# The delta rule without its matrix w: keys read the state, VectorE subtracts, one product with the inverse

## The reference, cut to what matters

```python
lower = where(strict, (k*beta) @ k.T * decay, 0)
rhs   = concat([v*beta, k*beta*exp(gc)])
u, w  = solve(lower + eye, rhs)          # the inverse applied to both halves
for c in chunks:                         # state is 128 x 128 per head
    v_new = u[c] - w[c] @ state
    o[c]  = q_dec[c] @ state + attn[c] @ v_new
    state = state * g_last[c] + k_dec[c].T @ v_new
```

## Time and profile before

| | |
|---|---|
| device time, median of 3 runs (lowest, highest) | 1108.64 us (1108.6, 1109.4) |
| span of the profiled execution | 1106.4 us |
| TensorE busy in it | 1086.0 us (98%) |
| VectorE, ScalarE, GpSimd busy | 603.2, 475.2, 480.6 us |
| head loop of the first mixer | from about 150 to 324 us; one head is 23.4 us |

### The profile page before, as it was taken

The page is one execution under the profiler, slowest core; times in us unless marked ns, Lnnn a source line. Parts: engine busy times, 40 slices in busy tenths (PEclk is TensorE's granted clock), DMA queues, the critical chain, the costliest instruction groups (busy, mean ns, idle before and its releaser), DMA issues. The chain is left out here.

```text
span 1106.4 us, 16476 instructions
## 1 busy us (share of the span) xinstructions
PE 1086.0 (98%) x5787; PEld 903.6 (82%) x5787; DVE 603.2 (55%) x1349; ACT 475.2 (43%) x1009; POOL 480.6 (43%) x276
## 2 busy tenths in 40 slices
PE   7999999999999999999999999999999999989996
PEld 6888899899988888888888888887788888767775
DVE  6677746666547555532122125536956666554667
ACT  6644345565534431431332234353434444454545
POOL 5785413222226684775575475356222122113130
PEclk9999999999999999999999999999999999999999
DMA  7544531211104444452541644604112011000011
GB/s 219 143 126 114 129 88 50 66 58 57 40 20 139 136 152 139 120 160 91 157 152 57 190 134 121 159 20 115 39 39 67 20 39 50 29 10 15 20 62 77
DMA packets 167158, 100.10 MB, mean 90 GB/s; under 512 B 30424, under 2 KB 160812, under 8 KB 166060
## 3 DMA queue, kind: packets, MB, share of 16 engines
q1 hardware_dynamic: 166924, 99.06, 31.1%
q10 hardware_dynamic: 160, 0.07, 0.0%
HBM read 95.69 MB, written 3.16 MB: 89 GB/s over the span
## 5 line engine op out<-in xcount | busy, mean ns | idle before, releaser
L1244 POOL TENSOR_TENSOR wlo<-stage,whi 128x1024 fp32r<-128x1024 f32 (+1 forms) x105 | 272.4, 2598 | 221.5 <-ACT whi L740 221.5
L2243 PE MATMUL ps<-hhi,whi 128*128 128x512 f32 (+1 forms) x728 | 311.5, 428 | 2.4 <-DVE gated L2005 1.9
L2243 PE MATMUL ps<-hhi,wlo 128*128 128x512 f32 (+1 forms) x728 | 294.0, 404 | 0.0
L2243 PE MATMUL ps<-hlo,whi 128*128 128x512 f32 (+1 forms) x728 | 285.1, 395 | 0.0
L2243 PEld LDWEIGHTS ps<-hhi,whi 128*128 128x128 f32 (+1 forms) x728 | 137.0, 188 | 37.3 <-issue 6.5
L2243 PEld LDWEIGHTS ps<-hhi,wlo 128*128 128x128 f32 (+1 forms) x728 | 137.3, 189 | 30.0 <-issue 6.3
L740 ACT ACTIVATE whi<-stage 128x1024 fp32r<-128x1024 f32 x104 | 109.7, 1056 | 121.0 <-PE ps L2243 89.0
L1342 POOL TENSOR_TENSOR wlo<-stage,whi 128x1024 fp32r<-128x1024 f32 (+3 forms) x40 | 73.4, 1835 | 194.3 <-ACT whi L1034 194.3
L2243 PEld LDWEIGHTS ps<-hlo,whi 128*128 128x128 f32 (+1 forms) x728 | 137.1, 188 | 24.0
L1122 ACT ACTIVATE prob<-ps,aneg 128x128 f32<-128x128 f32 (+1 forms) x96 | 50.9, 530 | 175.4 <-DVE aneg L2036 122.8
L2243 PE MATMUL ps<-ahi,whi 128*128 128x512 f32 x312 | 124.2, 398 | 0.0
(11 more groups left out here) (401 smaller groups left out, 1825.7 us busy)
## 6 DMA issues: line engine op xcount, KB each, us to landing
stage<-dn_w_in SPq DMA_DIRECT2D x32, 512.0 KB, 4.0
stage<-mlp_w_up SPq DMA_DIRECT2D x32, 512.0 KB, 4.3
stage<-mlp_w_down SPq DMA_DIRECT2D x32, 512.0 KB, 4.6
mod_w<-ada_w SPq DMA_DIRECT2D x8, 1536.0 KB, 6.5
stage<-w_in SPq DMA_DIRECT2D x17, 512.0 KB, 3.6
gcrow<-gc_rows SPq DMA_DIRECT2D x16, 256.0 KB, 3.5
stage<-dn_w_out SPq DMA_DIRECT2D x8, 512.0 KB, 3.6
stage<-w_in SPq DMA_DIRECT2D x9, 256.0 KB, 3.0
```

The lines of the kernel that those rows point to most:

```text
L1244: pool.tensor_tensor(wlo[:, slot, 0:ks, 0:cols], stage[:, slot, 0:ks, 0:cols], whi[:, slot, 0:ks, 0:cols], ALU.subtract).then_inc(s["w_lo" ...
L2243: mm = pe.matmul(bank, w[:, slot, k - ks[0], 0:width], x[:, k], start=(i == 0), stop=(i == len(todo) - 1))
```

## The change

w is not made any more: `w_product`, `w_out_`, `kbeta` and `wT` are gone. Instead, for each chunk c > 0, PE multiplies the keys by the state (`state_read`), DVE multiplies that by `kwgain` and subtracts `vbeta` (`less_read`, in place), and PE applies the inverse once (`v_new`); ACT's copy turns the sign. The head loop is written in another order on PE, ACT and DVE. The banks of finished projections are released after the taps and not after the silu.

```diff
+        def read_bank(h):
+            return 5 if h < H - 1 else 6
 ACT ----
-            def w_out_(g):
-                act.wait_ge(s["w_ps"], g + 1)
-                act.activation(wT[:, :, :], ps[:, 5, :].rearrange("p (c i) -> p c i", c=CH), ACT.Copy, scale=-1.0)\
-                    .then_inc(s["w_ev"], 1)
-
             def v_new(h, c):
                 act.wait_ge(s["v_ps"], h * 4 + c + 1)
-                act.activation(vnew[:, c, :], ps[:, 3, 0:P], ACT.Copy).then_inc(s["v_ev"], 1)
+                act.activation(vnew[:, c, :], ps[:, 3, 0:P], ACT.Copy, scale=-1.0 if c else 1.0).then_inc(s["v_ev"], 1)
 
             def o_first(h, c):
                 act.wait_ge(s["o1_ps"], h * 3 + c)
-                if h * 4 + c > 1:
+                if c > 1:
                     act.wait_ge(s["o_ready"], h * 4 + c)
+                elif h:
+                    act.wait_ge(s["o_ready"], h * 4)
...
                     tap0(f"q{g}")
+                o_first(h, 1)
+                v_new(h, 1)
+                if ahead:
+                    inv_32(g)
                     next_split(f"q{g}")
                 o_squares(h, 0)
-                v_new(h, 1)
-                if not ahead:
-                    out_hi(h - 1)
-                if ahead:
-                    inv_32(g)
-                o_first(h, 1)
+                o_first(h, 2)
+                v_new(h, 2)
                 if ahead:
                     conv_tanh(f"q{g}")
-                    q_squares(g)
+                    turned_64(g)
+                else:
+                    out_hi(h - 1)
                 o_squares(h, 1)
-                v_new(h, 2)
                 if ahead:
-                    turned_64(g)
-                o_first(h, 2)
-                if h and ahead:
-                    out_hi(h - 1)
-                o_squares(h, 2)
+                    tap0(f"v{g}")
+                o_first(h, 3)
                 v_new(h, 3)
                 if ahead:
-                    tap0(f"v{g}")
+                    q_squares(g)
                     next_split(f"v{g}")
                     conv_tanh(f"v{g}")
-                o_first(h, 3)
-                if ahead:
-                    w_out_(g)
+                    if h:
+                        out_hi(h - 1)
+                o_squares(h, 2)
                 o_squares(h, 3)
 DVE ----
-                dve.tensor_tensor(kbeta[:, :, :], kn, bc(kwgain[:, g], P), ALU.mult).then_inc(s["kside"], 1)
                 dve.tensor_tensor(kdec[:, :, :], kn, bc(gates[:, g, 2, :], P), ALU.mult).then_inc(s["kside"], 1)
...
+            def less_read(h, c):
+                dve.wait_ge(s["ks_ps"], h * 3 + c)
+                dve.wait_ge(s["vb_ready"], h + 1)
+                dve.scalar_tensor_tensor(out=vbeta[:, c], in0=ps[:, read_bank(h), 0:P], scalar=kwgain[:, h, c:c + 1], in1=vbeta[:, c],
+                                         op0=ALU.mult, op1=ALU.subtract).then_inc(s["rhs_ready"], 1)
...
+                less_read(h, 1)
                 out_rows(h, 0)
                 if ahead:
-                    taps(f"q{g}")
-                    inv_t_32(g)
-                else:
-                    out_gate(h - 1)
+                    taps(f"q{g}", (1, 2))
                 next_state(h, 1)
                 if ahead:
+                    taps(f"q{g}", (3,))
+                less_read(h, 2)
+                out_rows(h, 1)
+                if ahead:
+                    inv_t_32(g)
+                if h:
+                    out_gate(h - 1)
+                next_state(h, 2)
+                if ahead:
                     silu2(f"q{g}", qT[:, g % 2])
-                out_rows(h, 1)
-                next_state(h, 2)
-                if h and ahead:
-                    out_gate(h - 1)
+                less_read(h, 3)
                 out_rows(h, 2)
 PE ----
-            def w_product(g):
-                pe.wait_ge(s["l64_t"], g + 1)
-                pe.wait_ge(s["kside"], g * 2 + 1)
-                for c in range(CH):
-                    mm = pe.matmul(ps[:, 5, c * P:(c + 1) * P], kbeta[:, c], invT[:, g % 2, c], start=True, stop=True)
-                mm.then_inc(s["w_ps"], 1)
+            def state_read(h, c):
+                pe.wait_ge(s["st_ready"], h * 3 + c)
+                if h == H - 1:
+                    pe.wait_ge(s["attn_ready"], H)
+                pe.matmul(ps[:, read_bank(h), 0:P], chunk(kT[:, h], c), state[:, (c - 1) % 2], start=True, stop=True)\
+                    .then_inc(s["ks_ps"], 1)
...
-                elif c > 1:
-                    pe.wait_ge(s["o1_ev"], h * 3 + c - 1)
-                mm = pe.matmul(ps[:, 3, 0:P], invT[:, h % 2, c], vbeta[:, c], start=True, stop=(c == 0))
-                if c:
-                    pe.wait_ge(s["w_ev"], h + 1)
-                    pe.wait_ge(s["st_ready"], h * 3 + c)
-                    mm = pe.matmul(ps[:, 3, 0:P], wT[:, c], state[:, (c - 1) % 2], start=False, stop=True)
-                mm.then_inc(s["v_ps"], 1)
+                elif c:
+                    pe.wait_ge(s["o1_ev"], h * 3 + c)
+                    pe.wait_ge(s["rhs_ready"], h * 3 + c)
+                pe.matmul(ps[:, 3, 0:P], invT[:, h % 2, c], vbeta[:, c], start=True, stop=True).then_inc(s["v_ps"], 1)
...
                 o_rows(h, 0)
+                state_read(h, 1)
+                o_first(h, 1)
+                if ahead:
+                    level_32b(g)
+                fill(3)
                 v_new(h, 1)
-                if not ahead:
+                if h:
                     out_turn(h - 1)
-                if ahead:
-                    fill(2)
-                    level_32b(g)
-                fill(F_A if ahead else 3)
-                o_first(h, 1)
+                fill(F_A)
                 state_sum(h, 1)
                 fill(F_A)
                 o_rows(h, 1)
+                state_read(h, 2)
+                o_first(h, 2)
+                fill(3)
                 v_new(h, 2)
-                fill(2)
+                fill(3)
                 if ahead:
                     level_64a(g)
-                fill(F_A if ahead else 3)
-                o_first(h, 2)
                 state_sum(h, 2)
-                if h and ahead:
-                    fill(2)
-                    out_turn(h - 1)
                 fill(F_A)
                 o_rows(h, 2)
+                state_read(h, 3)
+                o_first(h, 3)
+                if ahead:
+                    level_64b(g)
+                fill(3)
                 v_new(h, 3)
                 if ahead:
-                    level_64b(g)
+                    k_rows(g)
                 fill(F_A)
-                if ahead:
-                    k_rows(g)
-                o_first(h, 3)
                 o_rows(h, 3)
                 fill(F_A)
                 if ahead:
                     qk_products(g)
-                    w_product(g)
                     q_sums(g)
```

More of the change, by code:

```diff
@@ L223, in build @@
         attnT = sb("attnT", [P, CH, P])
-        kbeta = sb("kbeta", [P, CH, P])
         kdec = sb("kdec", [P, CH, P])
         vbeta = sb("vbeta", [P, CH, P])
-        wT = sb("wT", [P, CH, P])
         vnew = sb("vnew", [P, CH, P])
@@ L351, in build @@
             lb_in lb_ps inv_step inv_out inv_in0 inv_in1 parts_ready inv_ready lev_ready base_ready
-            l32_ps l32_ev l32_r l32_inv l32_t l64_ps l64_ev l64_r l64_t kn_ps kside w_ps w_ev qk_ps attn_ready
+            l32_ps l32_ev l32_r l32_inv l32_t l64_ps l64_ev l64_r l64_t kn_ps kside ks_ps rhs_ready qk_ps attn_ready
             dmin q_sq qss_ps q_norm vn_ps vb_ready v_ps v_ev st_ps st_ready o_ps o1_ps o1_ev o_ready
@@ L916, in parts @@
                 if g >= 2:
-                    act.wait_ge(s["w_ps"], g - 1)
                     act.wait_ge(s["v_ps"], (g - 1) * 4)
@@ L933, in _ @@
             parts(1)
-            w_out_(0)
             for h in range(H):
@@ L1461, in _, with taps @@
             dve.tensor_scalar(V["dn_norm_w"], V["dn_norm_w"], 0.5 * float(P) ** -0.5, None, ALU.mult)
-            def taps(name):
+            def taps(name, which=(1, 2, 3)):
                 i, h, seq = CONV[name], int(name[1]), "qkv".index(name[0])
                 a, u = acc[:, i % 2], ps[:, bank_of_unit(name), :]
-                for t in range(1, 4):
+                for t in which:
                     dve.wait_ge(s["conv0"], i + 1) if t == 1 else dve.wait_ge(s["conv1"], i * 3 + t - 1)
@@ L2337, in consumed @@
                 else:
-                    pe.wait_ge(s["seq_ready"], CONV[name] + 1)
+                    pe.wait_ge(s["conv1"], CONV[name] * 3 + 3)
             def dn_unit(name):
@@ L2399, in fillers @@
                         if e < 2:
-                            pe.wait_ge(s["seq_ready"], CONV[("q7", "v7")[e]] + 1)
+                            pe.wait_ge(s["conv1"], CONV[("q7", "v7")[e]] * 3 + 3)
                         else:
-                            pe.wait_ge(*((s["w_ev"], H), (s["q_norm"], H))[e - 2])
```

(19 more changed lines are left out.)

## The result

The changed kernel takes 1115.9 us (median of 5 runs, 1114.9 to 1117.44) against 1108.64: a ratio of 1.0066, 95% interval 1.0055 to 1.0077. It is slower, by 7.3 us; the forecast was 1110.3 in a range up to 1113.1. The profiled execution has a span of 1115.6 us, 9.2 more than the one before.

The account below looks back on a forecast made before the run. TensorE was taken to bound the kernel, with no idle time in the head loop. -7.0 + 3.7 + 0.8 + 2.3 + 1.9 = +1.7 us on the 1106.4 span, median 2.2 above: 1110.3 us, range 1105.5 to 1113.1.

Parts of the forecast that it names:

- The clock falls (slower): Rival: TensorE's clock falls at the head 6 or end wait, +1.7 (1112.0), both 1113.7; swinging clock 1124; chance 0.14.
- the waits that I had counted: TensorE waits on o1, on vbeta, before k-tile 5 and before k-tile 7: +3.7, +0.8, +2.3 and +1.9 us.
- are as long as that pair, but with full work right up to them: New waits, 2.3 us (head 6) and 2.0 (end), compared with second-block idles of 1.89 and 0.82 us, where the clock fell.
- w products gone: TensorE: eight w products of 0.90 us removed, seven in the loop (6.3 us), 0.72 gained ahead of head 0: -7.0 us.
- v_new(h, 2) and v_new(7, 3) on o1: TensorE waits 0.41 us for ScalarE's copy to o1, behind less_read and out_rows, nine times: +3.7 us.
- v_new(h+1, 0) on vbeta: Four fillers instead of six ahead of the next head's first v_new; TensorE waits 0.12 us for vbeta, seven times: +0.8 us.
- k-tile 5 in head 6: Head 6's 40th filler, first needing head 5's output, waits for alo because ahi stands behind the tanh of v: +2.3 us.
- k-tile 7: After the last out_turn, 5 fillers instead of 13 cover the gf, ahi, alo chain; wait grows 0.1 to 1.97: +1.9 us.
- the rest of the new order: Other steps moved by a few fillers keep their cover; 64a, 64b and o_rows keep 0.2 to 1 us: no cost.
- level_32a of the next head none to spare: Next head's level_32a has no spare cover, put at nothing; missing it was part of a 0.15-chance rival, +1.4 to +2.8.
- no change that can be measured: Verdict on the whole kernel: 1110.3 us, 0.15% above 1108.64, within the 0.2% (2.2 us) that can't be told from no change.

Follow-up runs that it names:

- two buffers: Changed kernel with a second buffer for o1, chunks 1 and 3 in one and chunk 2 in the other: 1109.59 us.
- 10 fillers: Changed kernel with 10 instead of 15 fillers ahead of the last out_turn: 1113.07 us.
- ahi early: Changed kernel with ScalarE writing ahi right behind turned_64 instead of behind the tanh of v: 1114.97 us.
- tanh ahead of the split: Changed kernel with ahi right behind turned_64 and the tanh of v ahead of the split of the next weights on ScalarE: 1112.29 us.
- ahi early in head 6 alone: Changed kernel with ahi right behind turned_64 in head 6 (and head 7, as the change has it), other heads as in the change: 1113.01 us.
- w product twice: Kernel before the change with the w product run twice in each of the seven heads that prepare another: 1115.76 us.
- the version with four repairs: Changed kernel with ahi behind turned_64 in head 6, two o1 buffers, 10 fillers ahead of the last out_turn, 2 fillers moved behind v_rows: 1105.31 us.
- the wait ahead of q.k: Kernel before the change with one wait in head 6, by three squares on ScalarE, ahead of the q.k products: 1112.85 us.
- the two waits in the kernel before: Kernel before the change with k-tile 5 in head 6 waiting for ScalarE squares: six squares (about 2 us) 1113.33 us, three (about 1 us) 1111.4 us.
- best version: Changed kernel, ahi behind turned_64, tanh before split, two o1 buffers, 10 fillers before last out_turn, 2 fillers behind v_rows, out_base behind v_side: 1104.46 us.

## Why the prediction was wrong

The step that failed is the clock: the sum has it at nothing, and the rival "The clock falls (slower)" had 0.14 and "+1.7: 1112.0". It cost 3.4 us in head 6, which alone takes 1110.3 to 1113.7 and out of the range. A second step failed beside it: beyond the waits that I had counted, the sum puts the new order at nothing, and it cost 2.4 us. With the counted waits as forecast and a full clock that is 1112.7, inside the range but over the bound of what can be told from no change.

Of the clock, the mechanism was put in the right place, behind the wait in head 6; its chance was too low and its size was half of what came. That the waits "are as long as that pair, but with full work right up to them" was taken as a reason against it. Full work up to the wait did not help: in the changed kernel's head 6 the clock fell in all four profiles with a wait of 2.00 us there (the changed kernel twice, two buffers, 10 fillers), and once with 1.40 and once with 1.98. It did not with 1.74 ahead of the q.k products, with 1.0, and with 1.7 at the end of the loop in seven profiles; in three of these (ahi early, tanh ahead of the split, ahi early in head 6 alone) no fall in head 6 had gone before it. The price went by the one fall that the trace of before had shown, 3.4 us long; the four were 6.8 us, the other two 3.4.

The other terms, each against its measurement, as between A and C of the profiles:

| term | forecast | measured | from |
|---|---|---|---|
| w products gone | -7.0 | -7.0 | w product twice: 0.90 a head; A |
| v_new(h, 2) and v_new(7, 3) on o1 | +3.7 | +4.0 | two o1: 7 x 0.44 + 1.0 |
| v_new(h+1, 0) on vbeta | +0.8 | +0.8 | 22.80 to 22.68 a head (22.66 in the version with four repairs) |
| k-tile 5 in head 6 | +2.3 | +1.9 | 28.45 - 23.38, less the 3.2 of the clock's 3.4 that fall before head 7 |
| k-tile 7 | +1.9 | +1.8 | 10 fillers, and C-B |
| second head's level_32a, behind the silu of v in head 0 | 0 | +0.4 | 23.64 against 23.24 |
| the rest of the new order | 0 | +2.0 | 7 x 0.20, and 0.6 in C-B |
| clock in head 6 | 0 | +3.4 | windows, 6.8 us at 0.5 |
| sum | +1.7 | +7.3 | profiles up to C: +7.55 |

The w row takes the -0.7 ahead of head 0 from A: -0.47, while the start of the program came 0.2 us later in this execution. The rest of the new order: a head without any wait takes 22.68 us in the best version, not 23.38 - 0.90 = 22.48. No wait stands there; the 0.20 us lie in the spacing of starts. In head 3 the 48 fillers take 12.33 us instead of 12.22, and the six passes of the state read 0.67 where those of w times the state took 0.51. Why is open: the places where a filler gives way to a product are 13 in both. "level_32a of the next head none to spare" bound in the second head alone, where the silu of v had stood still beside wlo; with the tanh of v ahead of the split it took 0.69 us and the second head was as long as the others (23.53, 23.11 and 22.69 in three kernels).

The profiles differ by 9.2 us and the medians by 7.3, in the second batch by 8.5; that the first agrees with the sum up to C is chance, since the medians hold E-D too. The 1.56 us in E-D are not the change's. The instructions are the same in all kernels there, and their time is 110.54 without a fall of the clock (tanh ahead of the split), 111.2 to 112.2 with a fall of 3.4 us (before, head 6 alone, two buffers, the wait ahead of q.k) and 113.2 to 113.7 with one of 6.8, the w product twice and the two waits in the kernel before among them. So the forecast "no change that can be measured" failed by the 3.4 us of the clock and 2.4 of order, against a bound of 2.2; the price of the removed work and of the four waits was right to 0.4 us.

What stays open is what makes a fall 3.4 or 6.8 us long, and why 1.4 us of standing still brings one and 1.7 does not. The test with q.k behind the wait gave no fall in its profile, so it tells nothing on the length; its two groups of executions suggest that a part of it is chance. The Trainium skill, "TensorE: Matmul & The Clock Gate", section "What's actually happening", says that how many matmuls run at the lower clock at a kernel's start varies from run to run of the same kernel. It speaks of the start alone; these groups would be the same thing behind a wait, which no profile here shows.

## What to carry to other kernels

In a TensorE queue that is never idle a long wait can have a second price: behind 2 us of standing still in head 6 came 3.4 or 6.8 us of half clock, which cost 1.7 or 3.4 us, about as much as the wait itself or more. So after a reordering look for the one longest wait as well as for the sum of the short ones (here nine for 4.0 us, at full clock): a producer that moves back on a side engine (here ahi behind a tanh) may be harmless in five heads and cost 5 us in the sixth. The change paid only once the order around it was repaired: from +7.3 to -3.9 us with four repairs (ratio 0.9962) and to -4.8 with six (0.9956).

## What the runs showed of the hardware that was not expected

- A VectorE operation with both inputs in SBUF that is issued while GpSimd runs a long pass over SBUF stands still to its end: 4 columns took 1.66 instead of 0.15 us and ended 0.02 us after it, and the silu of v 2.36 instead of 0.69. Those with an input in PSUM kept their times beside it (attnT and vbeta 0.69 us, onat 0.28). The Trainium skill, "SBUF — State Buffer", section "Who interferes with whom", says this: a VectorE instruction with two SBUF inputs contends with a GpSimd instruction that reads SBUF, and one with at most one such input, outside the two-port modes, does not. The rows agree. The changed kernel meets it in head 0; from head 1 on its silu ends 1.1 us before wlo starts (192.52 and 193.62). In the kernel before wlo ends 0.16 us before the silu starts (167.93 and 168.09).
- The clock also falls where TensorE never stands still: in three profiles at 717, 720 and 727 us, around the MLP's norm, for 3.4 us, among them the best version's:

```profile
717.00:718.00 1.00, 1.00 (x8) 1.00 (x7) 0.18 (x1) 0.26 (x1) 1.00 (x1) 0.55 0.00 0
718.00:719.00 1.00, 1.00 (x6) 1.00 (x6) 0.00 (x0) 0.00 (x0) 1.00 (x2) 0.50 0.00 0
```

  D-C is 661.05 to 661.18 us there and 659.4 to 659.6 in the others. What runs ahead of it are products of one column and small ones without a reader; in the other 13 profiles the same instructions brought no fall.
